# Turning values and probability tiles in blocks through memory instead of on TensorE, in a two-layer hybrid attention encoder

## The reference

```python
kv = (ckv_all @ w_kv_up).reshape(b, n_keys, MLA_HEADS, MLA_NOPE + MLA_V)
...
logits = jnp.einsum('bqhmd,bkhmd->bmhqk', q, k2).astype(jnp.float32) * DIFF_SCALE + bias
logits = jnp.where(_chunk_mask(q_pos, k_pos), logits, -jnp.inf)
p = jax.nn.softmax(logits, axis=-1)
attn = (p[:, 0] - lam * p[:, 1]).astype(v.dtype)
return jnp.einsum('bhqk,bkhd->bqhd', attn, v)
```

## Time and profile before

| | us |
|---|---|
| median of 3 runs | 1643.68 (1642.51 to 1647.01) |
| the profiled execution, its time | 1643.9 |
| its span, first to last instruction | 1642.1 |
| PE busy | 1612.4 |
| DVE busy | 1202.8 |
| ACT busy | 902.5 |
| POOL busy | 903.1 |

### The profile page before, as it was taken

How to read it: one execution, slowest core, us unless ns; L and a number is a source line. 1 busy time by engine, 2 the same in 40 slices (tenths; PEclk the granted TensorE clock), 3 DMA queues, 4 the chain that set the end, 5 groups by cost and what they waited for, 6 DMA issues and landing times.

```text
span 1642.1 us, 32437 instructions
## 1 busy us (share of the span) xinstructions
PE 1612.4 (98%) x12028; PEld 1563.2 (95%) x12028; DVE 1202.8 (73%) x2233; ACT 902.5 (55%) x1776; POOL 903.1 (55%) x703
## 2 busy tenths in 40 slices
PE   9999999999999999999999999999999999999998
PEld 8989999999999999999999999899999999999997
DVE  5666655656656799889897789634357998898977
ACT  4365545454546665565565445644367655655654
POOL 4453445364544067677575547664450676775754
PEclk9999999999999999999999999999999999999999
DMA  6221223343422223423323332344242233233232
GB/s 189 81 64 53 67 78 86 77 108 77 112 75 68 65 78 92 115 71 111 97 84 90 89 81 70 92 120 110 64 110 60 78 94 112 74 107 98 84 91 71
DMA packets 283008, 145.50 MB, mean 89 GB/s; under 512 B 60591, under 2 KB 273261, under 8 KB 282853
## 3 DMA queue, kind: packets, MB, share of 16 engines
q1 hardware_dynamic: 278392, 136.27, 30.1%
q0 software_dynamic: 3616, 6.92, 1.6%
q10 hardware_dynamic: 844, 0.24, 0.1%
HBM read 130.69 MB, written 15.32 MB: 89 GB/s over the span
## 4 chain that ended last, share of the span: by engine, by line
PE 81%; DVE 11%; ACT 3%; issue 3%; POOL 1%; DMA 0%; POOLq 0%; ACTq 0%; DVEq 0%
PE ACC L1444 29%; PE ACC L1883 11%; PE ACC L1884 11%; PE ACC L1885 11%; PE ACC L1724 2%; PE S L1699 2%; PE S L1885 2%; PE S L1883 2%; PE S L1884 2%; DVE SCO L3137 2%; DVE TOP L3134 1%; PE T L1444 1%; ACT PR L2335 1%; PE T L1712 1%; PE S L1673 1%
## 5 line engine op out<-in xcount | busy, mean ns | idle before, releaser
L3645 POOL TENSOR_TENSOR WL<-RAW,WH 128x1024 fp32r<-128x1024 f32 (+3 forms) x89 | 187.8, 2114 | 147.2 <-ACT WH L2210 147.0
L1444 PE MATMUL ACC<-XGh,WH 128*128 128x288 f32 (+1 forms) x1008 | 227.6, 307 | 6.3 <-DVE XGl L2828 1.8
L1444 PE MATMUL ACC<-XGh,WL 128*128 128x288 f32 (+1 forms) x1008 | 215.3, 295 | 0.0
L1444 PE MATMUL ACC<-XGl,WH 128*128 128x288 f32 (+1 forms) x1008 | 215.3, 295 | 0.0
L1883 PE MATMUL ACC<-TB,WH 128*128 128x288 f32 x640 | 188.5, 295 | 1.4 <-DVE TB L3355 1.4
L1885 PE MATMUL ACC<-TB,WL 128*128 128x288 f32 x640 | 188.6, 295 | 0.0
L1884 PE MATMUL ACC<-TB,WH 128*128 128x288 f32 x640 | 188.3, 294 | 0.0
L2493 ACT ACTIVATE TC<-ACC 128x288 f32<-128x288 f32 x192 | 79.0, 411 | 167.7 <-PE ACC L1885 167.0
L1444 PEld LDWEIGHTS ACC<-XGh,WH 128*128 128x128 f32 (+1 forms) x1008 | 159.0, 188 | 11.4 <-issue 4.0
L1444 PEld LDWEIGHTS ACC<-XGh,WL 128*128 128x128 f32 (+1 forms) x1008 | 161.6, 188 | 0.0
L1444 PEld LDWEIGHTS ACC<-XGl,WH 128*128 128x128 f32 (+1 forms) x1008 | 161.3, 187 | 0.0
(11 more groups left out here) (517 smaller groups left out, 5244.2 us busy)
## 6 DMA issues: line engine op xcount, KB each, us to landing
RAW<-in_w_gate_dram SPq DMA_DIRECT2D x44, 512.0 KB, 3.9
RAW<-in_w_up_dram SPq DMA_DIRECT2D x44, 512.0 KB, 5.0
RAW<-in_w_down_dram SPq DMA_DIRECT2D x48, 384.0 KB, 3.8
RAW<-in_w_in_even_dram SPq DMA_DIRECT2D x29, 512.0 KB, 5.2
RAW<-in_w_in_odd_dram SPq DMA_DIRECT2D x28, 512.0 KB, 4.6
RAW<-in_w_out_even_dram SPq DMA_DIRECT2D x16, 512.0 KB, 4.2
RAW<-in_w_down_dram SPq DMA_DIRECT2D x16, 256.0 KB, 2.9
RAW<-in_w_out_odd_dram SPq DMA_DIRECT2D x8, 512.0 KB, 5.1
```

The source lines that it names most:

```text
L1444: ins = pe.matmul(out[0:m, 512 * b:512 * b + width], left, right[:, b * width:(b + 1) * width], start=(first and part == 0), stop=(last an ...
L3645: pool.tensor_tensor(WL[slot][:, 0:n], RAW[slot][:, 0:n], WH[slot][:, 0:n].bitcast(F32), ALU.subtract).then_inc(w_lo_pool, 1)
```

## The change

The keys' way of turning is used for the values of fifteen heads (8 to 15 and 17 to 23) and for probability tiles 2 and 3 of thirteen heads (8 to 14 and 17 to 22).

Values: DVE turns YV in 32x32 blocks into a new tile VT in slot 0; SP stores VT in eight transfers, straight to the value outputs; after its slot 7 SP waits for them and loads VF back from the outputs in two transfers. PE's five transpositions, their bank of T and DVE's two copies go.

Tiles 2 and 3: DVE turns the probabilities in blocks (PB) one slot after the scores; behind the load of VF, SP stores each in four transfers of 32 partitions to a part of `y_prompt` that is written only at the very end, waits for them and loads the turned tile (PF) in one; ACT writes the high halves (tile 2 at the end of slot 5, tile 3 in slot 7), POOL the low halves in the same slots. `weighted_values` waits for POOL's last low half. In heads after 8 with block values and a projection share in slot 1, the weighted values of the head before come after that share instead of in front of it.

```diff
+def blockwise(g):
+    return kind_of(g) != "mla" and g != 16
+BLOCK_TILES = (2, 3)
+BLOCK_HEADS = (8, 9, 10, 11, 12, 13, 14, 17, 18, 19, 20, 21, 22)
...
# SP, store_keys(g), behind the keys' eight transfers
+                if blockwise(g):
+                    sp.wait_ge(vals_made, value_loads(g) // 32 + 1)
+                    for name, b0, b1 in (("_prompt", 0, SEQ // SQUARE), ("_sample", SEQ // SQUARE, NT // SQUARE)):
+                        tokens = outs[dst + name][:, c].rearrange("(b t) (q d) -> q t b d", t=SQUARE, d=SQUARE)
+                        for q in range(QUADRANTS):
+                            sp.dma_start(tokens[q], VT[q * SQUARE:(q + 1) * SQUARE, b0:b1, :]).then_inc(vf_out, 16)
+                    return
...
+            def load_values(g):
+                sp.wait_ge(vf_out, value_stores(g + 1))
+                sp.wait_ge(job_lo, jobs.made("v", g - 1))
+                sp.dma_start(VF[:, 0:QT, :], outs[dst + "_prompt"][:, c].rearrange("(t p) d -> p t d", p=P)).then_inc(vf_in, 16)
+                sp.dma_start(VF[0:DEC, QT, :], outs[dst + "_sample"][:, c]).then_inc(vf_in, 16)
...
+            def store_blocks(h, t):
+                sp.wait_ge(pb_made, block_number(h, t) + 1)
+                for q in range(QUADRANTS):
+                    dst = bass.AP(place, first + q * SQUARE, [[P, SQUARE], [P * SQUARE, QUADRANTS * (t + 1)], [1, SQUARE]])
+                    sp.dma_start(dst, PB[t][q * SQUARE:(q + 1) * SQUARE, 0:(t + 1) * P].rearrange(
+                        "p (b q) -> p b q", q=SQUARE)).then_inc(pb_out[t], 16)
+            def load_turned(h, t):
+                sp.wait_ge(pb_out[t], 16 * QUADRANTS * (b + 1))
+                src = bass.AP(place, first, [[P, P], [P * P, t + 1], [1, P]])
+                sp.dma_start(PF[t][:, :, :], src).then_inc(pf_in[t], 16)
+            def turn_through_memory(h):
+                for t in BLOCK_TILES:
+                    store_blocks(h, t)
+                    if t > BLOCK_TILES[0]:
+                        load_turned(h, t - 1)
+                load_turned(h, BLOCK_TILES[-1])
...
# SP, attention(h), behind slot 7
+                if blockwise(h):
+                    load_values(h)
+                if h in BLOCK_HEADS:
+                    turn_through_memory(h)
...
# PE
+            def values_late(h):
+                c = share(h, 1)
+                return h > 8 and blockwise(h) and (c is None or c[3] < c[4])
...
             def weighted_values(h):
                 out = open_pair("pv", h)
                 pe.wait_ge(t_free, tr.made("p", h, QT))
+                if h in BLOCK_HEADS:
+                    pe.wait_ge(pf_lo, block_number(h, BLOCK_TILES[-1]) + 1)
...
-                    if 2 <= s < 2 + TOK_TILES and (h, s) != (16, 6):
+                    if 2 <= s < 2 + TOK_TILES and (h, s) != (16, 6) and not in_blocks(h, s - 2):
                         turn_probs(h, s - 2)
+                    if s == 1 and not blockwise(h):
+                        values_to_tokens(h)
                     if s == 1:
-                        values_to_tokens(h)
-                        if h % 16:
+                        if h % 16 and not values_late(h):
                             weighted_values(h - 1)
...
+                    if s == 1 and values_late(h):
+                        weighted_values(h - 1)
...
# ACT; called with (h, 3) in slot 7 and, behind the weight split, with (h, 2) in slot 5
+            def loaded_hi(h, t):
+                act.wait_ge(pf_in[t], 16 * (BLOCK_HEADS.index(h) + 1))
+                act.wait_ge(acc_done, acc.made("pv", h - 1))
+                act.activation(PTh[:, 0:t + 1, t * P:(t + 1) * P], PF[t][:, :, :], ACT.Copy).then_inc(pf_hi, 1)
...
# DVE
+            def turn_values(g):
+                dve.transpose(VT[:, :, :].rearrange("p b d -> p (b d)"), raw_values(g)[:, 0:NT]).then_inc(vals_made, 1)
+            def probs_to_blocks(h, t):
+                dve.wait_ge(*probs_made(h, t))
+                w = (t + 1) * P
+                dve.transpose(PB[t][:, 0:w], PR[0][:, n % 2, 0:w]).then_inc(pb_made, 1)
...
+                    if s and in_blocks(h, s - 1):
+                        probs_to_blocks(h, s - 1)
...
+                    if s == 0 and blockwise(h):
+                        turn_values(h)
...
# POOL; called with (h, 3) at the start of slot 7's work, with (h, 2) at the end of slot 5
+            def loaded_lo(h, t):
+                cols = slice(t * P, (t + 1) * P)
+                pool.wait_ge(pf_hi, block_number(h, t) + 1)
+                pool.tensor_tensor(PTl[:, 0:t + 1, cols], PF[t][:, :, :],
+                                   PTh[:, 0:t + 1, cols].bitcast(F32), ALU.subtract).then_inc(pf_lo, 1)
```

More of the change, by code:

```diff
@@ L148, in early_output, with value_stores, value_loads, in_blocks @@
     return h - 1 if h % 2 and kind_of(h) == "dsa" else None
+def blockwise(g):
+    return kind_of(g) != "mla" and g != 16
+def value_stores(g):
+    return 16 * sum(2 * QUADRANTS if blockwise(i) else 2 for i in range(8, g))
+def value_loads(g):
+    return 16 * 2 * sum(blockwise(i) for i in range(8, g))
+BLOCK_TILES = (2, 3)
+BLOCK_HEADS = (8, 9, 10, 11, 12, 13, 14, 17, 18, 19, 20, 21, 22)
+def in_blocks(h, t):
+    return h in BLOCK_HEADS and t in BLOCK_TILES
+def block_number(h, t):
+    return BLOCK_HEADS.index(h) * len(BLOCK_TILES) + BLOCK_TILES.index(t)
 def q_job_slot(g):
@@ L393, in plan_attention @@
             if s == 1:
-                tr.add("v", h)
-                tr.add("v5", h)
+                if not blockwise(h):
+                    tr.add("v", h)
+                    tr.add("v5", h)
                 if h % 16:
@@ L826, in build @@
         assert e <= own
+        (PB2, PF2, PF3), e = overlay(e, ("PB2", [P, 3 * P], F32), ("PF2", [P, 3, P], F32), ("PF3", [P, 4, P], F32))
+        assert e <= own
+        (PB3,), e = overlay(sq_off + size([P, NT], F32), ("PB3", [P, SEQ], F32))
+        PB, PF = {2: PB2, 3: PB3}, {2: PF2, 3: PF3}
         (QIh, QIl), end3 = overlay(end3, ("QIh", [P, 4, NT], F32R), ("QIl", [P, 4, NT], F32R))
@@ new lines, in load_turned @@
+            def load_turned(h, t):
+                b = BLOCK_HEADS.index(h)
+                sp.wait_ge(pb_out[t], 16 * QUADRANTS * (b + 1))
+                if b:
+                    sp.wait_ge(pf_lo, block_number(BLOCK_HEADS[b - 1], t) + 1)
+                place, first = turned_place(t)
+                src = bass.AP(place, first, [[P, P], [P * P, t + 1], [1, P]])
[6 more added lines that the diff above has]
+                load_turned(h, BLOCK_TILES[-1])
@@ L1284, in job_source @@
                 return acc_free, acc.made(w, g)
+            if w == "v" and blockwise(g):
+                return vf_in, value_loads(g + 1)
             if w == "v":
@@ L2329, in exponents @@
                 if n >= 2:
-                    act.wait_ge(t_done, tr.made("p", *divmod(n - 2, TOK_TILES)))
+                    before = divmod(n - 2, TOK_TILES)
+                    if in_blocks(*before):
+                        act.wait_ge(pb_made, block_number(*before) + 1)
+                    else:
+                        act.wait_ge(t_done, tr.made("p", *before))
                 if h == 16 and t == 0:
@@ L2376, in attention @@
                         job("k", g)
-                    if 2 <= s < 2 + TOK_TILES and (h, s) not in ((15, 5), (16, 4)):
+                    if 2 <= s < 2 + TOK_TILES and (h, s) not in ((15, 5), (16, 4)) and not in_blocks(h, s - 2):
                         turned_hi(h, s - 2)
+                    if s == 7 and h in BLOCK_HEADS:
+                        loaded_hi(h, 3)
                     if h in OUTPUT_FIRST and s == 2:
@@ L2431, in attention @@
                         job("k", g)
+                    if s == 5 and h in BLOCK_HEADS:
+                        loaded_hi(h, 2)
                     if s == 5 and h < 7 and h % 2 and h > 1:
@@ L3172, in attention @@
                         take_keys(h)
-                    if s == 1 and h != 16:
+                    if s == 0 and blockwise(h):
+                        turn_values(h)
+                    if s == 1 and not blockwise(h) and h != 16:
                         take_values(h)
@@ L3178, in attention @@
                         evacuate(("wo", *out_tile(h, s)), add_to_x(out_tile(h, s)[1]))
-                    if 2 <= s < 2 + TOK_TILES:
+                    if 2 <= s < 2 + TOK_TILES and not in_blocks(h, s - 2):
                         turned_lo(h, s - 2)
```

46 lines of the change are left out of this document (34 added, 12 removed).

## The result

The change makes the kernel slower: 1662.8 us (median of 4 runs, 1659.6 to 1664.7) against 1643.1 us (median of 4), a ratio of 1.0114 (95% interval 1.0093 to 1.0135). The forecast was 1643.0, its range 1631.5 to 1652.0, so the time lies outside, on the slower side. The profiled execution is the fastest of the four (1659.6 us, span 1657.8), so its span shows 15.7 us of the 19.7.

What follows compares the result with a forecast made beforehand. The prediction took TensorE (PE), busy 98% of the span, as the bound. From 1643.9 us it summed -14.7 (transpositions), +4.5 (POOL) and +9.3 (last heads) to -0.9, giving 1643.0, range 1631.5 to 1652.

Steps and rivals of the forecast that it cites:

- the order of the weighted values: Other diff heads: values of the head before come after a second projection share on PE; costed at nothing.
- The saving on PE: Transpositions leaving PE: 16.4 us at most over all heads, 14.7 of it up to head 22's value transpositions.
- DVE at nothing: VectorE's added block transpositions balance dropped copies and low halves; costed at nothing, with possible lateness of 0.5 to 0.7 us.
- POOL in heads 11, 13 and 15: Output tiles wait for GpSimd's MIX splits behind the new low halves: 1.5 us each, +4.5 (0 to 6.7).
- POOL in ordinary heads: Over the span POOL has room (55%); its queue was costed only at particular places, ordinary heads at nothing.
- its own sign: If ordinary heads wait for turned tiles, what the forecast costed at nothing is wrong.
- Heads 22 and 23: Memory round trips through SP's queue, without projections to cover them, delay the last value product by 9.3 us (6.7 to 11.9).
- the wait for the low halves of head 21 swallowed: POOL's late split delays head 21's values by 4 us, swallowed by the later wait since SP sets the end.
- Rival 2: Head 23's value round trip is slower: last product +17 us, in all +6.8 or 1650.7; chance 0.2.
- rival 3: The clock; its claim and size are cut from the given text; chance 0.07.
- Rivals 1 and 4: 1: round trips of heads 22, 23 hidden, 1632, chance 0.25. 4: PE not freed, up to 1652, chance 0.03.

Runs made afterwards that it cites:

- values_only: Changed kernel with no probability tile in blocks, only the values of fifteen heads through memory, weighted values in the changed order: 1650.1 us, ratio 1.0043.
- probs_only: Changed kernel with values turned on TensorE and weighted values where they were; only tiles 2 and 3 of thirteen heads through memory: 1655.5 us, ratio 1.0072.
- pause run: Kernel before, with PE waiting behind slot 2's scores for small memory transfers in heads 10, 12, 14, 18 and 20: 1685.7 us, ratio 1.0268.
- not_last: Changed kernel with heads 21 and 22 keeping their probability tiles on TensorE, and 22 and 23 their values: 1650.0 us, ratio 1.0045.
- out_first: Changed kernel with the output tile ahead of the weighted values in slot 1 of heads 9, 11, 13, 19 and 21: 1662.4 us, ratio 1.0120.
- split: Changed kernel with weighted values behind the first of three contraction tiles of slot 1's share in heads 9, 11, 13, 19, 21: 1654.8 us, ratio 1.0074.
- best: Changed kernel with low halves on VectorE, last heads' tiles and values on TensorE, weighted values late only in heads 18 and 20: 1641.3 us, ratio 0.9987.
- pe_values_23: Changed kernel with the values of head 23 alone turned on TensorE: 1659.2 us, ratio 1.0098.

## Why the prediction was wrong

**Where it failed: the order of the weighted values, costed at nothing.** The forecast has one half-sentence on it ("PE's values of the head before now come after a second projection share, so there I cost it at nothing"), which asked only who must be ready for the moved step. It did not ask what the moved step had stood next to. It costs 8.0 us by itself (5.7 to 9.9 by the interval). Nothing had to be run to see it: output tile and weighted values use one pair, and before had the share between them. With this term alone the forecast would have been 1651, within its range; what took the time past it are POOL in head 18 and VectorE, below, and some 4 us between executions.

**The saving on PE: right to about a tenth.** Between the starts of heads 8 and 22 PE's busy time fell from 927.3 to 915.6 us; without what the low clock adds (1.7 before, 3.3 after) that is 13.3, where the forecast had 14.7. Its price of 0.52 us for five value transpositions is that of a diff head; in head 22 they are 0.47.

**DVE at nothing: right for its work, not for its lateness.** Its level of work is the same (1197 against 1203 us), but the block transposition of tile 3 stands ahead of the mix of tile 4: 1.7 us more wait for PR in the diff heads, and 0.9 for STAT in head 8. The forecast named such a lateness, of 0.5 to 0.7, and gave it no term; it measured 2.6 us in all.

**POOL in heads 11, 13 and 15: right.** 3.1 us against 4.5, in the three heads and at the products named; within the ends.

**POOL in ordinary heads: missed.** This is what the forecast named as its own sign, ordinary heads that wait for turned tiles. It looked at POOL's queue at the diff pairs and at head 21, not at head 17, where the same order (bias loads, query split, weight split, then tile 3) puts the low half at 1079.93 and PE's product at 1081.47: 3.15 us of wait and 1.7 of clock, and 0.6 more for the keys at the start of head 18, which also come from POOL.

**Heads 22 and 23: the sum near, in part by luck.** 9.9 us against 9.3. But the 9.9 has three falls of the clock in it, 5.1 us in all, which the 9.3 hasn't. SP's queue for head 23 is as worked out, but for the 4.8 us by which head 22 starts later: sixteen stores from 1229.88 to 1237.86, the last load out at 1239.66, ACT's split at 1242.10, and the last value product 5.7 us behind it (forecast 5.5). But the forecast took head 23's values to be what sets the end. They alone are worth 4.0 us (values_only), the tiles alone 9.8 (probs_only). It also had the wait for the low halves of head 21 swallowed. In the trace that wait (4.43 us) is a link of the chain: tile 2 of head 22 is scaled and turned behind it, and SP stands idle from 1215.6 to 1219.8 before it can store blocks. With DVE making the low halves it is 2.8 us, and the end isn't earlier (42.1 us from the start of head 22), because waits for X and PR grow in its place; what it costs by itself isn't shown. Rival 2 put the last product 17 us after that of before with PE held at head 22, 7 more than it is.

**The clock: rival 3, too rare in the odds.** It had 0.07. Four falls came that before doesn't have, three of them in the last two heads, 1.7 each and 6.9 in all. Each long wait should have had its price with it: two of the steps summed ended in waits of 4 us. The trace of before has no wait of several us, but the forecast overlooked that the clock had fallen there at 540, behind a wait of only 1.17 us. The clock fell behind a wait of 3.15 us here and behind all five pauses of the pause run, 3.9 us and longer. The length of the wait alone doesn't decide: not_last and out_first had waits of 3.13 and 3.28 us at the same place and kept 1.00.

**Rivals 1 and 4.** Hidden transfers: in the ordinary heads they are, but that was not where the time went. That PE is not freed: no.

In one sum from the start of head 8 to that of head 22: -13.3 off PE, +7.3 order, +3.1 MIXl, +3.2 PTl in head 18 with 1.7 of clock and 0.6 for the keys, +2.6 DVE: +5.2, against 5.1 measured.

Since the profiled execution shows 15.7 of 19.7 us, some of the difference is between executions: the other runs of the changed kernel had a mean clock of 0.991 to 0.992, this one 0.994. On a span of 1660 us that is 3 to 5 us more, if PE had work all the while.

## What to carry to other kernels

When a step is moved, ask what it now stands next to, not only who waits for it: two users of one accumulator need something between them about as long as the evacuation (DVE's two BO copies, 1.0 us here), and swapping them doesn't help (1662.4 us against 1662.8); splitting the work that stood between does (1654.8). Price a long wait of TensorE at its length plus what the clock takes behind it: 1.6 to 1.9 us behind the pauses, and up to 4.7 (in split). A round trip through memory was hidden in heads of 32 to 36 us with projections in them, and cost about 10 us in the last two, where nothing is left to hide it: leave it out there.

## What the runs showed of the hardware

- In best, VectorE's subtraction out of SBUF took longer while GpSimd subtracted out of SBUF too: 0.68 us with GpSimd idle, 2.6 to 2.9 us when started within 0.8 us of the start of GpSimd's. The DVE instruction at 1071.95 ended at 1074.80, 0.56 us after POOL's that ended at 1074.24. Where two of POOL's followed each other without a gap (the row at 364.88 with x2), DVE's, started at 365.68 during the first, ended only 0.57 us after the second.
- The clock fell behind short waits too, and not each time: behind 1.17 us at the end of layer 0's attention in six of the sixteen profiled executions, before's among them, and in head 8, behind waits of 1.05 and 0.74 us that followed each other closely, in three (best, values_only, pe_values_23) of the twelve that have these waits. What decides between a fall and none isn't shown.
- The change adds 96800 packets (379808 against 283008), 85152 of them under 512 B, and in the attention none of PE's longer waits is released by a transfer. The block stores of 64 KB landed in 1.9 us (median), the loads of 256 KB in 2.8.
